# Attention's keys without zero rows: scores that contract over a head's own 64 partitions

## What is computed

```python
q = rms_norm(q.reshape(b, s, 16, 64), q_norm[i])
k = rms_norm(k.reshape(b, s, 16, 64), k_norm[i])
y_att = dilated_attention(q, k, v)      # three dilations, causal windows
# per head and branch:
scores = jnp.einsum("bnqrhe,bnkrhe->bnrhqk", qb, kk) * (1.0 / math.sqrt(64))
p = exp(scores - m); o = einsum(p / sum(p), vv)
```

## Time and profile before

| | us |
|---|---|
| median of three runs | 2077.96 |
| lowest and highest | 2070.40, 2078.97 |
| the profiled execution | 2082.28 |
| its span, first to last instruction | 2080.5 |
| TensorE matmuls busy | 2038.0 (98%) |
| VectorE busy | 1694.0 (81%) |
| ScalarE busy | 1226.4 (59%) |
| mean granted clock of TensorE | 0.995 |

### The profile page before, as it was taken

One profiled execution on the slowest core, in us unless ns is written; L12 is line 12 of the kernel. 1 busy time (PEld: TensorE's weight loads), 2 busy tenths in 40 slices (PEclk: granted clock), 3 DMA queues, 4 the chain that ended last, 5 costly groups with the idle time before them and its releaser, 6 DMA issues. The chain is left out here.

```text
span 2080.5 us, 37945 instructions
## 1 busy us (share of the span) xinstructions
PE 2038.0 (98%) x14911; PEld 1888.4 (91%) x14911; DVE 1694.0 (81%) x2099; ACT 1226.4 (59%) x1539; POOL 477.5 (23%) x254
## 2 busy tenths in 40 slices
PE   8999999999999999999999999999999999999997
PEld 8999999999999999999999999999877777777775
DVE  5788868668777887868667757998799999999998
ACT  5344665653335335666653346444478888888886
POOL 4895000008922991000008910000000000000000
PEclk9999999999999999999999999999999999999999
DMA  8875554257765775554347853445579999999994
GB/s 251 283 258 179 180 155 151 83 174 250 252 212 194 261 242 172 163 163 142 102 163 243 271 191 114 139 133 193 216 291 370 361 368 369 370 361 369 366 366 182
DMA packets 238941, 483.74 MB, mean 233 GB/s; under 512 B 10612, under 2 KB 178976, under 8 KB 222464
## 3 DMA queue, kind: packets, MB, share of 16 engines
q1 hardware_dynamic: 226880, 443.58, 60.9%
q0 software_dynamic: 11360, 37.21, 5.4%
q10 hardware_dynamic: 608, 1.65, 0.2%
HBM read 481.31 MB, written 1.09 MB: 232 GB/s over the span
## 5 line engine op out<-in xcount | busy, mean ns | idle before, releaser
L818 PE MATMUL misc<-xhl,ring_low 128*128 128x256 f32 x1568 | 435.9, 278 | 0.0
L817 PE MATMUL misc<-xhl,high_b 128*128 128x256 f32 x1376 | 383.5, 279 | 1.0 <-ACT xnT L1968 1.0
L819 PE MATMUL misc<-xhl,high_b 128*128 128x256 f32 x1376 | 382.2, 278 | 0.0
L818 PEld LDWEIGHTS misc<-xhl,ring_low 128*128 128x128 f32 x1568 | 294.6, 188 | 0.8
L3290 DVE TENSOR_TENSOR ring_low<-ring,high_b 128x2048 fp32r<-128x2048 f32 x128 | 287.1, 2284 | 0.6 <-issue 0.6
L2556 DVE TENSOR_TENSOR ring_low<-ring,high_b 128x2048 fp32r<-128x2048 f32 x92 | 263.3, 2901 | 14.1 <-ACT high_b L1911 13.8
L817 PEld LDWEIGHTS misc<-xhl,high_b 128*128 128x128 f32 x1376 | 260.1, 189 | 2.3 <-ACT xnT L1968 1.2
L819 PEld LDWEIGHTS misc<-xhl,high_b 128*128 128x128 f32 x1376 | 258.3, 188 | 0.0
L2277 ACT ACTIVATE high_b<-ring 128x2048 fp32r<-128x2048 f32 x124 | 235.7, 1914 | 35.7 <-DMA ring<-in_w_dram 35.0
L1801 POOL TENSOR_SCALAR arena<-arena,cact 128x1024 f32<-128x1024 f32 x56 | 212.8, 3801 | 3.5 <-DMA arena<-in_w_ada_f_dram 0.7
L1557 PE MATMUL misc<-high_b,u_rows 128*128 128x512 f32 x512 | 204.2, 399 | 1.8 <-DVE u_rows L3333 1.2
(11 more groups left out here) (493 smaller groups left out, 5564.0 us busy)
## 6 DMA issues: line engine op xcount, KB each, us to landing
ring<-in_w_dram SPq DMA_DIRECT2D x128, 1024.0 KB, 8.0
ring<-in_w_in_dram SPq DMA_DIRECT2D x72, 1024.0 KB, 5.4
ring_d<-in_w_dram SPq DMA_DIRECT2D x128, 512.0 KB, 5.0
ring<-in_ffn_w_gate_dram SPq DMA_DIRECT2D x44, 1024.0 KB, 5.4
ring<-in_ffn_w_up_dram SPq DMA_DIRECT2D x44, 1024.0 KB, 9.1
ring_d<-in_ffn_w_down_dram SPq DMA_DIRECT2D x88, 512.0 KB, 7.1
arena<-in_w_ada_dram POOLq DMA_DIRECT2D x48, 512.0 KB, 4.9
ring<-in_w_out_dram SPq DMA_DIRECT2D x20, 1024.0 KB, 4.9
```

The source lines that it names most:

```text
L817: pe.matmul(dst, wh, ml, start=start, stop=False, **kw)
L818: pe.matmul(dst, wl, mh, start=False, stop=False, **kw)
L819: return pe.matmul(dst, wh, mh, start=False, stop=stop, **kw)
```

## The change

The keys are kept as [128, 8, 256] in the first eight blocks of `xc`, two heads in the 128 partitions, as q is. The two zero copies and the wait in front of them go. Each key fill is copied by one instruction of 128 partitions instead of two of 64, on the same engine and with the same semaphore. `scores` takes 64 partitions of q and of the keys, 0 to 63 for even heads and 64 to 127 for odd ones. Number, order, waits and column counts of TensorE's matmuls stay as they were.

```diff
--- before.py
+++ after.py
@@ -287,7 +287,7 @@
         at[0] = max(after, at[0])
         here = at[0]
         xc = part([NX, SEQ])
-        keys2 = xc.rearrange("p (e k) s -> p e k s", e=2)
+        keysT = xc[:, 0:KD, :]
         after = at[0]
         at[0] = here
         xdec = part([D])
@@ -1206,7 +1206,8 @@
                 n0 = RING["wout", l]
 
                 def scores(h):
-                    q, k = turned_q(h // 2), keys2[:, h % 2, h // 2, :]
+                    hs = slice(h % 2 * HD, (h % 2 + 1) * HD)
+                    q, k = turned_q(h // 2)[hs], keysT[hs, h // 2, :]
                     b = claim_bank(m0 + AF["S", h])
                     pe.matmul(b[:, 0:P], q[:, 0:P], k[:, 0:P], start=True, stop=True)
                     pe.matmul(b[:, P:3 * P], q[:, P:SEQ], k, start=True, stop=True).then_inc(filled, 1)
@@ -2081,12 +2082,6 @@
                     if j == 0:
                         high_w_block(15)
                     if j == 3:
-                        wait_filled(act, FILL["off", l] + 1)
-                        flat_keys = keys2.rearrange("p e k s -> p (e k s)")
-                        act.activation(flat_keys[HD:P, 0:KD * SEQ], ident[HD:P, 0:1].to_broadcast([HD, KD * SEQ]),
-                                       ACT.Copy)
-                        act.activation(flat_keys[0:HD, KD * SEQ:], ident[0:HD, HD:HD + 1].to_broadcast([HD, KD * SEQ]),
-                                       ACT.Copy)
                         act.wait_ge(gated, l + 1)
                         for g in range(GROUPS):
                             ins = act.activation(xdt[:, 0, g * BLK:(g + 1) * BLK], xtok[:, 0, g * BLK:(g + 1) * BLK],
@@ -2113,11 +2108,8 @@
                 for q in range(2):
                     m = FILL["qkt", l] + 4 + q
                     wait_filled(act, m)
-                    for e in range(2):
-                        hs = slice(e * HD, (e + 1) * HD)
-                        ins = act.mul(keys2[hs, e, 2 * q:2 * q + 2, :],
-                                      bank_of(m)[hs, :].rearrange("p (a b) -> p a b", a=2), cola[hs, l, C_KN:C_KN + 1])
-                    ins.then_inc(drained[m % 4], 1)
+                    act.mul(keysT[:, 2 * q:2 * q + 2, :], bank_of(m).rearrange("p (a b) -> p a b", a=2),
+                            cola[:, l, C_KN:C_KN + 1]).then_inc(drained[m % 4], 1)
 
             def out_high_piece(l, k):
 
@@ -2867,12 +2859,8 @@
                 for q in range(2, 4):
                     m = FILL["qkt", l] + 4 + q
                     wait_filled(dve, m)
-                    for e in range(2):
-                        hs = slice(e * HD, (e + 1) * HD)
-                        ins = dve.tensor_scalar(keys2[hs, e, 2 * q:2 * q + 2, :],
-                                                bank_of(m)[hs, :].rearrange("p (a b) -> p a b", a=2),
-                                                cola[hs, l, C_KN:C_KN + 1], None, ALU.mult)
-                    ins.then_inc(drained[m % 4], 1)
+                    dve.tensor_scalar(keysT[:, 2 * q:2 * q + 2, :], bank_of(m).rearrange("p (a b) -> p a b", a=2),
+                                      cola[:, l, C_KN:C_KN + 1], None, ALU.mult).then_inc(drained[m % 4], 1)
 
             def out_low_piece(l, k):
```

## The result

| | before | after |
|---|---|---|
| median of 20 runs each, us | 2079.15 | 2086.07 |
| lowest and highest, us | 2070.40, 2088.27 | 2080.61, 2095.25 |
| profiled execution and its span, us | 2082.28, 2080.5 | 2093.04, 2091.3 |

The kernel became slower: the ratio is 1.0032, with a 95% interval of 1.0018 to 1.0046. Of 2079.15 us that is 6.7 us, 3.7 to 9.6. The forecast was 8.4 us, 1.0040.

What follows compares the result with a forecast made beforehand. The prediction took TensorE's stream as the bound and summed 0 (zero copies) - 2.9 (key copies) + 11.3 (64-row scores) = +8.4 us, from the median 2077.96 to 2086.4 us; range 2073 to 2092.

Steps and rivals of the forecast that it cites:

- What bounds: Whole kernel: TensorE is busy 2038.0 of 2080.5 us, so the attention stage's gain or loss there moves the end.
- Part 1: ScalarE's two zero copies per layer, removed: 3.8 us per layer turn into idle time behind the v projection, gain 0.
- Part 2: Key copies before the scores, four pairs becoming four single ones per layer: 1.46 us gained per layer, 2.9 in all.
- Part 3: Scores over 64 partitions: 64 switches between 64-row and 128-row products stall weight loads, a loss of 11.3 us.
- entering: TensorE going from 128-row products into a head's 64-row scores: 0.20 us lost each time, 16 times per layer.
- leaving: TensorE going from 64-row scores back to 128 rows: 0.15 us lost before transposes, 0.19 before output rows.
- the leap from 16 rows to 64: Scores on TensorE: assumes 64-row products stall the next load as the traced 16-row ones did; chance 0.68.
- the border term: Stalled weight loads where TensorE's scores switch row count: 64 switches, 5.7 us per layer, 11.3 in both.
- No border at 64 rows: Rival for the scores: switching to 64 rows costs nothing, leaving -2.9 us, 2075.1 us; chance 0.22.
- Loads inside a head stall too: Rival for the scores: three more stalled loads per head at 0.20 us, 19 us more, 2105.6 us; chance 0.04.
- Half the time for half the height: Rival for the scores: half-height products run in half their time, -13.4 us in sum, 2064.6 us; chance 0.03.

Runs made afterwards that it cites:

- the 96-row run: Kernel before, with even heads' scores contracting over 96 partitions (64 of their own, 32 zero) and odd heads' over 128; 2079.14 us, 83.03 us per layer in the stretch.
- part 3 alone: Kernel before, with only the scores contracting over 64 partitions; both key arrays, zero copies and paired key copies stay; ratio 1.0056.

## Why the prediction was right, point by point

**What bounds.** Right. TensorE is busy throughout the stage, and what its stream gained or lost showed up whole: 8.6 us in the stretches, 6.7 (3.7 to 9.6) in the medians. That the ratio's middle is 1.9 us lower than the stretches is within its interval, and no run here separates them.

**Part 1, 0.** Right, shown by leaving the zero copies out alone. The cover was the one named, the v projection.

**Part 2, -2.9.** Right: 2 x 1.50 = 3.0 where it was done alone, inside the bounds of 2.7 to 3.1. The row of transposes without a gap was foretold, and so was the place of the first scores. They begin at 368.96, and 5.08 of that is the shift which was already there at the first q transpose, so 363.88 on before's clock, against "near 363.8". The single copy of 128x512 took ScalarE 0.72 us, not the 0.70 of the q copies, and VectorE 0.75.

**Part 3, +11.3.** Right: 2 x 5.77 = 11.5 where it was done alone, 11.6 in the whole change (2 x 4.30 + 3.0). The sum was not right by errors that cancel: the terms held one by one, entering 0.19 against 0.20, leaving 0.15 and 0.19 as forecast. (The forecast's own formula for entering, 0.28 - 0.07 + 0.10 - 0.12, gives 0.19; I had put it up to 0.20.) The price came from two borders that the earlier trace rows showed at 16 rows and 16 columns, from the overlap in the earlier trace rows and the exposed load in the earlier trace rows. The step that could have failed was the leap from 16 rows to 64, which no row of before could settle and to which I gave 0.68. It held, and the 96-row run shows where it would have failed: with 96 rows the border term would have been 0.

**The rivals.** "No border at 64 rows" would have needed the loads to begin with the products; they begin 0.07 ahead of the end. "Loads inside a head stall too" fell: only the first load of a head has idle time in front of it. The four products of a head start 0.21, 0.11 and 0.22 us apart in the trace of part 3 alone (374.599, 374.813, 374.924, 375.143), where the 0.21 holds the exposed load that the price of entering already counts. "Half the time for half the height" was wrong as I put it (one product by itself takes 377 ns), but it pointed at something true which I had given up too early. I wrote that the trace doesn't bear the speedup out because 16-row products follow one another at the full pitch. Those eight all use the same rows. Products in different rows are another case, and the change as made never puts two of these side by side.

## What to carry to other kernels

In this kernel a half-height matmul between full-height ones gave nothing and cost two borders of about 0.18 us each. It pays once the other half has a partner next to it, with one border in and one out for both, and with a bank of its own free in time. Zeros in the unused half were the better choice while the products stood alone: they keep the stream without borders, and making them cost nothing on the path. What that layout did cost is the copies of the keys in pairs, 1.5 us per layer. When a pair needs two banks at once, look for the waits that this makes before judging the pairing, and move just enough independent work in front of each wait; moved everywhere, it made new waits.

## What the runs showed of the hardware that was not expected

- Matmuls over partitions 0 to 63 and 64 to 127 run side by side in fp32 even if each half's matmuls are issued in a block of their own: starts 13 ns apart, 0.87 us for eight where four take 0.85. The records don't name the partitions, so that the second of each two belongs to the second head is my reading. That a product of the second head starts ahead of one that the program issued before it needs no reading: all four products of L1213 start before any of L1214, at every pair, and at full height the same program keeps its order. Whether the chip or the compiled program makes this order, no run here tells. The Trainium skill, TensorE: Matmul & The Clock Gate, The mechanism, has products start strictly in the order of the program; these starts speak against it, if the compiled program keeps the order of the source.
- A change between 128 rows and 96 is no border (load 0.37 us ahead of the end, stage +0.02 us), as one to 114 isn't; one to 64 is, as one to 16 is the earlier trace rows.
- The load behind a border begins 0.071 to 0.073 us ahead of the recorded (modelled) end of the last product, at all 64 borders of the kernel after.
